# Chunked mLSTM by pairs of heads in a two-layer hybrid block on one Trainium2 core

## What is computed

```python
b_cum = jnp.cumsum(fc, axis=-1)
logd = jnp.where(tril, b_cum[..., :, None] - b_cum[..., None, :] + ic[..., None, :], NEG)
inter = b_cum + m[..., None]
m_t = jnp.maximum(inter, jnp.max(logd, axis=-1))
sc = jnp.einsum('bhtd,bhsd->bhts', qc, kc) * jnp.exp(logd - m_t[..., None])
w_inter = jnp.exp(inter - m_t)
num = jnp.einsum('bhts,bhsv->bhtv', sc, vc) + w_inter[..., None] * jnp.einsum('bhtd,bhdv->bhtv', qc, c_mat)
den = jnp.sum(sc, axis=-1) + w_inter * jnp.einsum('bhtd,bhd->bht', qc, n_vec)
h_t = num / jnp.maximum(jnp.abs(den), jnp.exp(-m_t))[..., None]
# state: c_new = carry * c_mat + einsum('bhs,bhsd,bhsv->bhdv', w, k, v), n_new alike
```

## Time and profile before

| | us |
|---|---|
| median of 3 runs | 2063.19 (2059.76 to 2066.58) |
| the profiled execution | 2068.53 |
| its span, first to last instruction | 2066.6 |
| TensorE busy | 1933.5 (94%) |
| VectorE / ScalarE / GpSimd busy | 634.6 / 623.6 / 616.3 |
| mean granted TensorE clock | 0.943 |

### The profile page before, as it was taken

How to read it: one execution, slowest core, us unless ns; L and a number is a source line. 1 busy time by engine, 2 the same in 40 slices (tenths; PEclk the granted TensorE clock), 3 DMA queues, 4 the chain that set the end, 5 groups by cost and what they waited for, 6 DMA issues and landing times.

```text
span 2066.6 us, 25293 instructions
## 1 busy us (share of the span) xinstructions
PE 1933.5 (94%) x10168; PEld 1522.8 (74%) x10168; DVE 634.6 (31%) x1221; ACT 623.6 (30%) x850; POOL 616.3 (30%) x360
## 2 busy tenths in 40 slices
PE   4999989998978999999999969999998969999997
PEld 2888756676857888888888837775666748888885
DVE  2134165454353111111101256202566351111114
ACT  1522223443334321122111244324342353222123
POOL 0442201000434333222222453431010454434343
PEclk8999999999988999999999979996777989999998
DMA  7421134001343222122211162220002343323321
GB/s 272 112 62 52 52 102 140 24 1 38 96 143 111 61 61 81 41 65 67 72 53 54 56 196 61 62 78 25 1 0 76 88 141 100 105 82 109 89 79 49
DMA packets 210361, 163.12 MB, mean 79 GB/s; under 512 B 17669, under 2 KB 190949, under 8 KB 210277
## 3 DMA queue, kind: packets, MB, share of 16 engines
q1 hardware_dynamic: 207744, 157.77, 25.4%
q10 hardware_dynamic: 2532, 4.18, 0.6%
HBM read 159.83 MB, written 2.10 MB: 78 GB/s over the span
## 4 chain that ended last, share of the span: by engine, by line
PE 84%; DVE 7%; ACT 3%; issue 2%; DMA 2%; POOL 1%; ACTq 0%; DVEq 0%; SPq 0%
PE ps L585 56%; PE ps L998 4%; PE ps L983 3%; PE ps L573 2%; PE ps L575 2%; PE ps L574 2%; PE ps L789 2%; PE ps L741 2%; PE ps L766 2%; PE ps L682 1%; DMA ring<-in_mod_w 1%; PE ps L698 1%; DVE xT L1617 1%; DVE xT L1627 1%; PE ps L776 1%
## 5 line engine op out<-in xcount | busy, mean ns | idle before, releaser
L1872 POOL TENSOR_TENSOR wlo<-ring,whi 128x1024 fp32r<-128x1024 f32 (+1 forms) x136 | 317.1, 2344 | 576.5 <-ACT whi L1227 576.3
L585 PE MATMUL ps<-hlo,whi 128*128 128x512 f32 (+1 forms) x1152 | 348.8, 357 | 0.0
L585 PE MATMUL ps<-hhi,whi 128*128 128x512 f32 (+1 forms) x1056 | 324.3, 361 | 10.4 <-DVE modc L1412 8.3
L585 PE MATMUL ps<-hhi,wlo 128*128 128x512 f32 (+1 forms) x1056 | 319.4, 357 | 0.0
L585 PEld LDWEIGHTS ps<-hlo,whi 128*128 128x128 f32 x1152 | 192.5, 190 | 34.6
L585 PEld LDWEIGHTS ps<-hhi,whi 128*128 128x128 f32 x1056 | 175.3, 190 | 39.7 <-DVE modc L1412 8.3
L585 PEld LDWEIGHTS ps<-hhi,wlo 128*128 128x128 f32 x1056 | 173.8, 189 | 30.5
L1675 DVE TENSOR_TENSOR hu<-sg,ps 128x768 f32<-128x768 f32 (+1 forms) x44 | 36.1, 821 | 510.4 <-ACT sg L1239 510.4
L1227 ACT ACTIVATE whi<-ring 128x1024 fp32r<-128x1024 f32 (+1 forms) x136 | 135.0, 1024 | 177.6 <-PE ps L585 176.1
L585 PE MATMUL ps<-uhi,whi 128*128 128x512 f32 (+1 forms) x528 | 160.8, 359 | 0.0
L1590 DVE SCALAR_TENSOR_TENSOR xT<-ps,modc,xT 128x512 f32<-128x512 f32 x96 | 60.6, 659 | 325.0 <-PE ps L585 217.4
(11 more groups left out here) (255 smaller groups left out, 2868.6 us busy)
## 6 DMA issues: line engine op xcount, KB each, us to landing
ring<-in_mod_w SPq DMA_DIRECT2D x96, 512.0 KB, 5.0
ring<-in_ffn_w_in SPq DMA_DIRECT2D x88, 512.0 KB, 3.8
ring<-in_ffn_w_out SPq DMA_DIRECT2D x32, 512.0 KB, 3.6
ring<-in_m_w_in SPq DMA_DIRECT2D x24, 512.0 KB, 3.7
ring<-in_ab_w_in SPq DMA_DIRECT2D x21, 512.0 KB, 4.0
ring<-in_ffn_w_out SPq DMA_DIRECT2D x16, 384.0 KB, 3.2
ring<-in_ab_w_out SPq DMA_DIRECT2D x8, 512.0 KB, 5.1
ring<-in_m_w_out SPq DMA_DIRECT2D x8, 512.0 KB, 5.7
```

The costliest lines, as they stand in the source:

```text
L585: mm = pe.matmul(dst[:, a:b], w, h[:, a:b], start=st, stop=sp_)
L1872: pool.tensor_tensor(wlo[:, s, 0:width], ring[:, (NB[f"ffn{l}"] + s) % RING, 0:width], whi[:, s, 0:width].bitcast(F32), ALU.subtract).then ...
```

## The change

The context and the four latent tiles are now chunks of 128. Scores are computed for the diagonal 128x128 blocks alone; everything earlier enters by a state of 64x129 per head, direction and tile. Heads go in pairs (`NP` = 4): the heads of a pair sit on partitions 0 to 63 and 64 to 127. For pair p TensorE transposes the keys (`key_rows`), spreads the negative maxima of each head (`max_rows`) and the query weights of both (`query_rows`), by selection matrices in fp32r whose rows hold high and low parts (`selx`, `nx`, `qx`), makes the scores (`m_scores`), the state updates (`m_updates`) and the outputs (`m_values(i)`, i one tile of a pair). VectorE weighs keys (`m_keys`), queries (`m_queries`) and scores (`m_weigh`), runs the states over the tiles (`m_states`) and inverts denominators. ScalarE now also scales the numerators (`m_numerators`); GpSimd masks four blocks in one operation, adds both directions (`m_add_both`) and normalises the first three pairs (`m_normalise`).

New rows are prepared in the projection: VectorE forms exponents `wr` (key weights) and `qr` (query weights) after the last convolution, ScalarE exponentiates and copies them, GpSimd clears `qx` and `nx`, and TensorE transposes `li`, the floor and `wr` between the two halves of the value projection instead of after the projection. The mod14 units come after all values.

```diff
@@ TensorE, input projection
         token_major("in1", 8, [(t, t) for t in (4, 5, 0, 1, 2, 3)], *in1_parts, lambda b: pe.wait_ge(f_ev, (7, 8, 6)[b // 2]))
-        v1 = {3: lambda: pe.wait_ge(gate_ev, 4), 0: lambda: pe.wait_ge(vg_ev, 1), 1: lambda: pe.wait_ge(vg_ev, 2)}
+        pe.wait_ge(gate_ev, 4)
+        pe.wait_ge(rows_ok, 1)
...
+        pe.wait_ge(wr_exp, 1)
+        for d in range(2):
+            for t in range(TT):
+                at = (4 * LT + d * TT + t) * H_M
+                mm = pe.transpose(half(7)[:, at:at + H_M], wr[0:H_M, d, t * P:(t + 1) * P], ident[0:H_M, 0:H_M])
+        mm.then_inc(tr_mm, 1)
@@ TensorE, pairs
+        def m_scores(p):
+            pe.wait_ge(mexp, 4 * p + 4)
+            for c in range(LT):
+                for b in range(2):
+                    rows, cols = slice(M_DK * b, M_DK * (b + 1)), slice(c * P, (c + 1) * P)
+                    mm = pe.matmul(half(b)[:, cols], mk[rows, p, cols], mq[rows, p, cols], start=True, stop=True)
+            mm.then_inc(m_s, 1)
+        def m_updates(p):
+            pe.wait_ge(m_q, p + 1)
+            pe.wait_ge(m_p, p + 1)
+            for d in range(2):
+                for n in range(LT):
+                    js = (LT, LT + 1) if n == 0 else (order_tile(d, n - 1),)
+                    bank, at = (half(2 + d), (M_DV + 1) * n) if n < LT - 1 else (half(0), (M_DV + 1) * d)
+                    for j in js:
+                        for b in range(2):
+                            rows = slice(M_DK * b, M_DK * (b + 1))
+                            mm = pe.matmul(bank[rows, at:at + M_DV + 1], kw[:, p % 2, d, j, rows], mv[:, j, 2 * p + b, :],
+                                           start=(j == js[0]), stop=(j == js[-1]))
+            mm.then_inc(m_u, 1)
...
+        for p in range(1, NP + 1):
+            i = LT * (p - 1)
+            if p < NP:
+                key_rows(p)
+                max_rows(p, 0)
+            m_values(i)
+            if p < NP:
+                query_rows(p)
+                max_rows(p, 1)
+            m_values(i + 1)
+            if p < NP:
+                m_scores(p)
+            m_values(i + 2)
+            if p < NP:
+                m_updates(p)
+            m_values(i + 3)
+        mod_rows(1, 4, PS[0])
+        mod_columns(1, 4, PS[0])
@@ ScalarE, after the floor's exponential and ahead of the splits 10 to 13
+        act.wait_ge(wr_in, 1)
+        act.activation(wr[0:H_M, 0, 0:LAT - P], wr[0:H_M, 0, 0:LAT - P], ACT.Exp)
+        act.activation(wr[0:H_M, 1, P:LAT], wr[0:H_M, 1, P:LAT], ACT.Exp)
+        act.activation(wr[0:H_M, :, LAT:T], wr[0:H_M, :, LAT:T], ACT.Exp).then_inc(wr_exp, 1)
+        act.wait_ge(qr_in, 1)
+        step(act.activation(qr[0:H_M, :, :], qr[0:H_M, :, :], ACT.Exp))
...
@@ ScalarE, pairs
+        def m_numerators(i):
+            act.wait_ge(m_den, i + 1)
+            if i >= 2:
+                act.wait_ge(m_add, i - 1)
+            for b in range(2):
                 for d in range(2):
...
+                    ins = act.activation(hbt[:, i % 2, b, d, :], out_bank(i)[:, at:at + M_DV], ACT.Copy,
+                                         scale=dab[:, i % 2, b, d:d + 1])
+            ins.then_inc(m_num, 1)
...
+        for p in range(1, NP + 1):
+            i = LT * (p - 1)
+            if p < NP:
+                m_exps(p, 0)
+            m_numerators(i)
+            if p >= 2:
+                m_inverse_std(p - 2)
+            if p < NP:
+                m_exps(p, 1)
+            for q in range(1, LT):
+                m_numerators(i + q)
@@ VectorE, pairs
+        def m_states(p):
+            dve.wait_ge(m_u, p + 1)
+            for n in range(LT):
+                for d in range(2):
...
+                        ins = dve.scalar_tensor_tensor(stt_[:, p % 2, d, n, :], stt_[:, p % 2, d, n - 1, :], dcol[:, p % 2, d, q:q + 1],
+                                                       new, ALU.mult, ALU.add)
+                if n < LT - 1:
+                    step(ins)
+            ins.then_inc(m_st, 1)
@@ GpSimd, pairs
+        def m_add_both(i):
+            p, c = divmod(i, LT)
+            pool.wait_ge(m_num, i + 1)
...
+            pool.tensor_tensor(dst, hbt[:, i % 2, :, 0, :], hbt[:, i % 2, :, 1, :], ALU.add).then_inc(m_add, 1)
```

More of the change, by code:

```diff
@@ L109, in shape_constants @@
     for h in range(H_M):
-        k[h, K_SEL + h * P:K_SEL + (h + 1) * P] = 1.0
+        for row in (h, SPLIT_ROW + h):
+            k[row, K_SEL + h * P:K_SEL + (h + 1) * P] = 1.0
+            half_at = K_SEL2 + h // 2 * P + M_DK * (h % 2)
+            k[row, half_at:half_at + M_DK] = 1.0
     return k
@@ new lines, in m_values, with dst @@
+        def m_values(i):
+            p, c = divmod(i, LT)
+            if i < 2:
+                pe.wait_ge(vg_ev, 8)
+            else:
+                pe.wait_ge(m_num, i - 1)
+            if c == 0:
+                pe.wait_ge(m_st, p + 1)
+            cols = slice(c * P, (c + 1) * P)
+            def dst(b, d):
+                at = 512 * b + (M_DV + 1) * d
+                return out_bank(i)[:, at:at + M_DV + 1]
+            for d in range(2):
+                n = order_tile(d, c)
+                for b in range(2):
+                    rows = slice(M_DK * b, M_DK * (b + 1))
+                    pe.matmul(dst(b, d), qs[rows, p % 2, d, cols], stt_[rows, p % 2, d, n, :], start=(d == 0), stop=False,
+                              skip_group_check=True)
+            for d in range(2):
+                for b in range(2):
+                    mm = pe.matmul(dst(b, d), pe_[:, p % 2, b, d, cols], mv[:, c, 2 * p + b, :], start=False, stop=True,
+                                   skip_group_check=True)
+            mm.then_inc(m_o, 1)
@@ new lines, in _ @@
+        ins.then_inc(wr_in, 1)
+        for d in range(2):
+            at_ctx = gt[0:H_M, d, ctx_end[d]:ctx_end[d] + 1]
+            e3 = ends[d].unsqueeze(2).broadcast_to((H_M, LT - 1, P))
+            dve.tensor_tensor(by_tile(qr[0:H_M, d, later[d]]), by_tile(negm[0:H_M, d, later[d]]), e3, ALU.add)
+            ins = dve.tensor_scalar(qr[0:H_M, d, first[d]], negm[0:H_M, d, first[d]], at_ctx, None, ALU.add)
+        ins.then_inc(qr_in, 1)
+        dve.wait_ge(qx_hi, 1)
+        dve.tensor_tensor(qx[SPLIT_ROW:NROW, :, :], qr[0:H_M, :, :], qx[0:H_M, :, :].bitcast(F32), ALU.subtract).then_inc(qx_lo, 1)
@@ new lines, in _ @@
+        m_states(0)
+        for p in range(1, NP + 1):
+            i = LT * (p - 1)
+            if p < NP:
+                m_keys(p)
+            m_denominators(i)
+            if p >= 2:
+                step(m_stats(i - 1))
+                m_aggregate(p - 2)
+            if p < NP:
+                m_queries(p)
+            m_denominators(i + 1)
+            m_stats(i)
+            if p < NP:
+                m_weigh(p)
+            m_denominators(i + 2)
+            m_stats(i + 1)
+            if p < NP:
+                m_states(p)
+            m_denominators(i + 3)
+            m_stats(i + 2)
@@ L1934, in _ @@
+        m_select(0, 0)
+        m_select(0, 1)
+        for p in range(1, NP + 1):
+            i = LT * (p - 1)
+            if p < NP:
+                m_select(p, 0)
+            m_add_both(i)
+            if p < NP:
+                m_select(p, 1)
+            for q in range(1, LT):
+                m_add_both(i + q)
+            if p >= 2:
+                m_normalise(p - 2)
         out_projection(1, wsp_out1)
```

361 lines of the change are left out of this document (209 added, 152 removed).

## The result

The changed kernel takes 1991.5 us (median of 4 runs, 1989.1 to 2006.5), the kernel before 2064.9 in the same runs: ratio 0.966, 95% interval 0.961 to 0.971. The forecast was 1994, between 1970 and 2025.

What follows compares the result with a forecast made beforehand. TensorE's queue bounds the kernel before; afterwards one chain through the engines bounds the stage. Stage -73.7, outside it +0.2, +3.7 and +1.0, together -68.8 us, giving 1994 us against the median of 2063.19; range 1970 to 2025.

Steps and rivals of the forecast that it cites:

- the stage: From the first key transposes to the end of the last product: 183.2 us before, forecast 109.5, so -73.7.
- the end: Last part of the stage, from the last pair's values through denominators, numerators, statistics and subtractions to the product: 21.4 us.
- rival 2: Clock is up in most of the stage, so TensorE's links halve: -21 us, 1973; chance 0.15.
- the new stage has no such run: In the stage, no value-matmul run of some 10 us, which had raised the clock, so 1.2 GHz was taken throughout.
- Halves of the array side by side: In the stage's paired-head matmuls, row groups and column groups both overlap, each by a factor of two.
- Rival 1: In the stage, row groups do not overlap: some 16 us more, 2010; with columns serial too, 2027; chance 0.25.
- Normalising a pair, 5 us on GpSimd, lies beside: In the stage, GpSimd's normalising takes 5 us per pair and runs beside the chain.
- (b): In the projection, seven ScalarE instructions ahead of its tenth weight split delay TensorE: +3.7 us, between 0 and 6.
- (a): Gate-row transposes move from the gap ahead of the stage to between the value projection's halves: net +0.2 us.
- (c): Last mod weights are asked for after all values, some 3 us later against them: +1.0 us, between 0 and 3.
- Rival 3: GpSimd and VectorE collide beside VectorE's chain, six to ten collisions of 2 us: 2006 to 2014; chance 0.10.
- Rival 4: The same collision at each small VectorE operation on SBUF alone makes the kernel slower; 40 would give 2074; chance 0.02.

Runs made afterwards that it cites:

- the second profile: The changed kernel, unchanged, profiled again on the same chip: stage 107.5 us, and 767.4 us from the gate projection to the end.
- the exchanged loops: Against the changed kernel, scores, updates and state part of the values do all of one head, then the other: stage 116.2 us.

## Why the prediction was right, step by step

- **What bounds, and by how much the stage shrinks**: right, 109.0 for 109.5 (107.5 in the second profile). But the sum was right by luck, by two errors that cancel. Measured against forecast: pair 0 21.6 for 19.9, pair 1 18.9 for 20.8, pairs 2 and 3 19.8 and 21.0 for 23.7 each, the end 27.8 for 21.4. My own sign of being wrong, a middle pair under 20 us, came true with 18.9 and 19.8: the sum of a middle pair failed in the term of the clock, and the end in the term of normalising, both below.
- **Durations of single operations**: mostly right. Eight exponentials 2.2 for 2.2, four weighings 2.5 for 2.6, numerators 1.1 for 1.1, Ln and Exp with loads 3.1 for 3.0, keys 1.8 for 1.8, states 2.4 for 2.1, an add of 256 columns 0.72 for 0.8, a mask 0.64 for 0.75. Forgotten: the table load of the first exponentials, 1.28 in pair 0's chain.
- **The clock**: wrong. I took 0.50 throughout; it was 0.54 in pair 0, 0.73 in pair 1 (0.90 in the second profile) and over 0.9 in pairs 2 and 3 (0.83 in the second profile's pair 2). The updates there took 2.4 for 4.3, transposes and values shrank alike, while the scores, which stand behind a wait of 4.0 us, stayed at 2.1 in pair 2; my rival 2 was half true. The step that failed is "the new stage has no such run": the group of values and updates was enough, and the run with extra matmuls shows that idling, not half-filled rows, is what lowers it.
- **Halves of the array side by side**: right for columns and rows, by the exchanged loops. Rival 1 falls. (Its price was summed too high: with the six value groups of my own sum it is 6.8 + 5.2 = 12 us, not 16.) What a change of mode costs was not tried apart; in the trace the first two steps from the state matmuls (64 rows) to the value matmuls (128) are 0.20 and 0.21 us, the next ones 0.11, so at most 0.2 a group, 3 us over the stage. That is about the 3.5 us that I had estimated by the rule of the Trainium skill, TensorEngine Tiling (Array Packing), Key Properties.
- **"Normalising a pair, 5 us on GpSimd, lies beside"**: wrong, the largest single miss. It is 8.6 us, and it lies ahead of the masks and sums of pair 3 and of the last product in the same queue. That made +6.4 at the end, and pair 3 lasted 21.0 us where pair 2 lasted 19.8. I had priced GpSimd's work and not asked what stands behind it on its queue.
- **Outside the stage (b)**: right in place, half in size. ScalarE's seven instructions took 5.8 for 6.1, but VectorE's convolutions ended 1.1 us later, counted from the gate projection, and 2 us later against TensorE's queue, which had itself come 0.9 us earlier (why isn't shown). Behind the 5.27 us wait came 2.2 us of lower clock: 7.5 for 3.7, 7.4 to 8.0 given back when undone. (a) The 28 transposes took 1.8 for 2.6 and one of two waits of 0.78 went, but the gap ahead of the stage stayed: 3.86 us, all of it ScalarE's four sigmoids, where before 2.03 and the transposes filled the same time. So +1.0 for +0.2; 7.5 + 1.0 - 0.9 leaves the measured +7.8 within 0.2. (c) No loss: 464.7 behind the stage instead of 468.1, in both pairs of profiles, where I had +1.0. These 3.4 us lie in the out projection and the FFN, 1 us here and there; what gives them isn't shown.
- **The sum**: -74.2 + 7.8 - 3.4 = -69.8 from the gate projection on, for -68.8. Outside the stage, too, two errors cancel: +7.8 for +3.9 ahead of it, -3.4 for +1.0 behind it. The medians differ by 73.4; the pace of the single execution, worth up to 10 us, is in them.
- **Rival 3, collisions**: seen, but not in the pairs: VectorE's last product 3.34 for 1.22 beside GpSimd's split of the out weights, and in the run in which VectorE normalises. Rival 4 did not come near: reciprocals 0.18 in the stage, where VectorE and GpSimd both worked.

## What to carry to other kernels

When work is spread over more engines, price each engine's queue at its last place, not its busy time: a filler that is "beside" the chain by its busy time is in the chain as soon as the chain's own next step stands behind it in that queue, in pair 3 as at the end. Where a chain has idle gaps on TensorE, the clock is a term of the sum of its own, of either sign, and behind a long wait some microseconds at the lower level belong to the wait's price (2.2 us behind one of 5.27). Where the levels fall also varies between executions of one kernel, here by 1.6 us. Single edits that each shorten a chain of four engines don't add, since the next engine is never far behind; measure them together before counting them.

## What the runs showed of the hardware that I had not expected

- The same code ran at two paces at a granted clock of 1.00: 1133 to 1135 or 1155 to 1156 matmul records in 200 us of the same FFN, from execution to execution of the changed kernel and its variants, 11 us by the end of that FFN; the FFN of layer 1 has 884 or 885 records in 200 us in both profiles of the changed kernel.
- TensorE starts a matmul on the other half of the rows while up to three records of the first half are still ahead of it in the queue, so matmuls do not all start in the order of the program; for groups of two matmuls interleaving by hand gave nothing (0.72 us in both orders).
- After a wait of 5.27 us eleven fp32r matmuls of 512 columns followed each other by 0.43 us instead of 0.23.
- A product of VectorE on 8 columns lasted 2.26 us beside a subtraction of GpSimd on 1024, instead of 0.17.
